# Differences of differential attention and the normed state space output turned by transposing DMAs instead of TensorE

## What is computed

```python
def _ssd_branch(z, ...):                   # y: the state space output, 1024 channels, 2 groups
    yg = (y * jax.nn.silu(z.astype(f32))).reshape(bsz, s, SSD_GROUPS, SSD_WIDTH // SSD_GROUPS)
    yg = yg * lax.rsqrt(jnp.mean(yg * yg, axis=-1, keepdims=True) + EPS)
    return (yg.reshape(bsz, s, SSD_WIDTH) * norm_g.astype(f32)).astype(z.dtype)

def _diff_branch(q, k, v, ...):            # 8 heads, blocks of 128 queries
        sc = jnp.einsum('bqhtd,bkhtd->bhtqk', qi, k) * (HEAD_DIM ** -0.5)
        p = jax.nn.softmax(jnp.where(mask, sc, -jnp.inf), axis=-1)
        attn = p[:, :, 0] - lam * p[:, :, 1]
        return jnp.einsum('bhqk,bkhe->bqhe', attn.astype(v.dtype), v)
```

## Time and profile before

| | |
|---|---|
| median of 3 runs | 1940.49 us (1938.78 to 1941.45) |
| the profiled execution's own time | 1941.98 us |
| its span in the trace | 1940.2 us |
| PE busy | 1914.1 us (99%), granted clock 0.999 |
| DVE busy | 1180.9 us (61%) |
| ACT busy | 996.3 us (51%) |
| POOL busy | 389.1 us (20%) |
| share of the 16 DMA engines | 33.9% |

### The profile page before, as it was taken

One profiled execution on the slowest core, in us unless ns is written; L12 is line 12 of the kernel. 1 busy time (PEld: TensorE's weight loads), 2 busy tenths in 40 slices (PEclk: granted clock), 3 DMA queues, 4 the chain that ended last, 5 costly groups with the idle time before them and its releaser, 6 DMA issues.

```text
span 1940.2 us, 28236 instructions
## 1 busy us (share of the span) xinstructions
PE 1914.1 (99%) x11272; PEld 1044.9 (54%) x11272; DVE 1180.9 (61%) x1555; ACT 996.3 (51%) x1924; POOL 389.1 (20%) x266
## 2 busy tenths in 40 slices
PE   7999999999999999999999999999999999999998
PEld 4446755455455665544454576554554556655443
DVE  6677555587436877644367765655872477775432
ACT  5674454465324666533356644544662256665321
POOL 0212011142212232111001130112331222321110
PEclk9999999999999999999999999999999999999999
DMA  6224223343334443233222242233333443332421
GB/s 190 86 87 153 98 98 109 98 117 96 103 103 126 125 126 109 88 130 137 66 66 87 77 163 94 103 109 91 111 104 109 125 115 105 114 109 88 156 93 44
DMA packets 204525, 208.98 MB, mean 108 GB/s; under 512 B 28688, under 2 KB 193514, under 8 KB 204394
## 3 DMA queue, kind: packets, MB, share of 16 engines
q1 hardware_dynamic: 204394, 207.17, 33.9%
HBM read 181.91 MB, written 2.16 MB: 95 GB/s over the span
## 4 chain that ended last, share of the span: by engine, by line
PE 91%; DVE 3%; issue 2%; ACT 1%; DMA 1%; POOL 1%; SPq 0%; DVEq 0%; POOLq 0%; ACTq 0%
PE PS L558 89%; DVE X L1315 1%; PE PS L750 1%; PE PS L666 1%; DVE wsp L1312 1%; DMA stage<-w_in 1%; PE PS L798 0%; PE PS L806 0%; POOL X L1672 0%; PE PS L836 0%; DMA X<-X 0%; DVE Y L1312 0%; DVE Y L1471 0%; ACT Y L1210 0%; DVE M L1312 0%
## 5 line engine op out<-in xcount | busy, mean ns | idle before, releaser
L558 PE MATMUL PS<-hT,wsp 128*128 128x512 f16 (+2 forms) x4968 | 1085.7, 376 | 1.0 <-ACT hT L966 1.0
L558 PEld LDWEIGHTS PS<-hT,wsp 128*128 128x128 f16 x4968 | 479.1, 98 | 556.4 <-issue 11.9
L1312 DVE SCALAR_TENSOR_TENSOR wsp<-stage,wsp 128x2048 f16<-128x2048 f32 x148 | 352.9, 2385 | 165.5 <-ACT wsp L985 163.3
L558 PE MATMUL PS<-ys,wsp 128*128 128x512 f16 x1536 | 340.4, 379 | 0.0
L985 ACT ACTIVATE wsp<-stage 128x2048 f16<-128x2048 f32 x148 | 281.3, 1901 | 50.6 <-PE PS L558 46.9
L558 PEld LDWEIGHTS PS<-ys,wsp 128*128 128x128 f16 x1536 | 149.4, 98 | 177.0 <-issue 4.1
L558 PE MATMUL PS<-wsp,hT 128*128 128x256 f16 x1728 | 194.2, 273 | 0.0
L558 PEld LDWEIGHTS PS<-wsp,hT 128*128 128x128 f16 x1728 | 168.5, 98 | 22.7 <-issue 2.3
L988 ACT ACTIVATE X<-PS 128x512 f32<-128x512 f32 (+1 forms) x120 | 68.5, 594 | 143.4 <-PE PS L558 122.9
L1672 POOL TENSOR_TENSOR X<-X,K 128x1024 f32<-128x1024 f32 x26 | 63.8, 2452 | 365.5 <-DMA X<-X 365.5
L1001 ACT ACTIVATE G<-PS,halfA 128x512 f32<-128x512 f32 x64 | 43.9, 686 | 161.2 <-PE PS L558 119.1
(11 more groups left out here) (199 smaller groups left out, 2056.9 us busy)
## 6 DMA issues: line engine op xcount, KB each, us to landing
stage<-w_in SPq DMA_DIRECT2D x120, 1024.0 KB, 4.9
stage<-w_branch SPq DMA_DIRECT2D x32, 1024.0 KB, 5.0
X<-X SPq DMA_DIRECT2D x120, 128.0 KB, 2.3
stage<-w_out SPq DMA_DIRECT2D x8, 1024.0 KB, 5.4
Y<-sums SPq DMA_DIRECT2D x8, 512.0 KB, 5.8
M<-sums SPq DMA_DIRECT2D x8, 512.0 KB, 5.7
Y<-Y SPq DMA_DIRECT2D x24, 128.0 KB, 2.3
xres<-x SPq DMA_DIRECT2D x4, 512.0 KB, 6.5
```

What stands on the lines that cost most here:

```text
L558: return pe.matmul(o, a, b, start=start, stop=stop, skip_group_check=True)
L1312: return dve.scalar_tensor_tensor(out=o, in0=a, scalar=c, in1=b, op0=op0, op1=op1)
```

## The change

Both uses of PE transposes go. The differences are written in place (dE), rounded on ACT to a high half and on DVE to a low half side by side in a new f16 buffer dH, and one DMA for each block `n`, issued by SP, transposes both halves at once: 2(i+1) squares of 128 x 128 in f16. For the state space output, DVE now multiplies by the reciprocal norm and by the channel weight, which lies along the free axis as a row loaded to all partitions (`norm_row`); ACT and DVE write the halves into the memory of xs[g], and two DMAs for each group transpose 16 squares each. That memory of group 1 is also used by the first rotated query panel, so ACT waits for all four DMAs (`yb_in`) before it empties slot 28's first bank.

```diff
@@ SP: new
+                def turn_differences(p):
+                    for e in range(2):
+                        n = 2 * (p - DIFF0) + e
+                        halves = 2 * (n % 4 + 1) * P
+                        sp.wait_ge(s["df_hi"], at("df_hi", n + 1, layer))
+                        sp.wait_ge(s["df_lo"], at("df_lo", n + 1, layer))
+                        if n >= 2:
+                            sp.wait_ge(s["df_o"], at("df_o", n - 1, layer))
+                        sp.dma_start_transpose(dPT[:, e, 0:halves].rearrange("p (b n) -> p b n", n=P), dH[:, e, 0:halves])\
+                            .then_inc(df_turned[e], 16)
...
+                def turn_normed(g):
+                    sp.wait_ge(s["yb_hi"], at("yb_hi", g + 1, layer))
+                    sp.wait_ge(s["yb_lo"], at("yb_lo", g + 1, layer))
+                    sp.wait_ge(s["y_lo"], at("y_lo", 8, layer))
+                    for h, y in enumerate((Y_HI[1], Y_LO[1])):
+                        sp.dma_start_transpose(y[:, 4 * g:4 * g + 4, :].rearrange("p t (c n) -> p (t c) n", n=P), turned_z[g][h])\
+                            .then_inc(s["yb_in"], 16)
...
+                    if DIFF0 <= p - 2 < DIFF0 + 16:
+                        turn_differences(p - 2)
+                    if p - 2 in SSD_END:
+                        turn_normed(SSD_END[p - 2])
@@ PE
-                            pe.wait_ge(s["df_a"], at("df_a", n + 1, layer))
-                            for b in range(n % 4 + 1):
-                                last = pe.transpose(PS[:, 4 + 2 * e, P * b:P * b + P], dA[:, e, P * b:P * b + P], ident)
-                            last.then_inc(s["df_T"], 1)
...
-                        pe.wait_ge(s["ssd_norm"], at("ssd_norm", g + 1, layer))
-                        pe.wait_ge(s["ssd_y"], at("ssd_y", 4 * g + 4, layer))
-                        for t in range(4):
-                            for c in range(ST):
-                                last = pe.transpose(PS[:, 4 + t, c * P:c * P + P], z[g][:, c, t * P:t * P + P], ident)
...
-                            pe.wait_ge(s["df_Tl"], at("df_Tl", n + 1, layer))
+                            pe.wait_ge(df_turned[e], at("df_turned0", 16 * (n // 2 + 1), layer))
@@ ACT, ahead of evacuate(p, 0)
+                            act.wait_ge(s["df_a"], at("df_a", n + 1, layer))
+                            if n >= 2:
+                                act.wait_ge(df_turned[e], at("df_turned0", 16 * (n // 2), layer))
+                            copy(dH[:, e, 0:nk], dE[:, e, 0, 0:nk]).then_inc(s["df_hi"], 1)
...
+                        if kind == "qc" and i == 0:
+                            act.wait_ge(s["yb_in"], at("yb_in", 64, layer))
@@ DVE
-                        tt(z[g], z[g], grin.unsqueeze(2).to_broadcast([P, ST, S]), ALU.mult).then_inc(s["ssd_norm"], 1)
+                        for c in range(ST):
+                            last = stt(z[g][:, c, :], z[g][:, c, :], grin[:, c:c + 1], norm_row, ALU.mult, ALU.mult)
...
+                            tt(dH[:, e, nk:2 * nk], dE[:, e, 0, 0:nk], dH[:, e, 0:nk], ALU.subtract).then_inc(s["df_lo"], 1)
```

More of the change, by code:

```diff
@@ L265, in program @@
         sy = X[:, 4096:4608].rearrange("p (e u n) -> p e u n", e=2, u=2)
-        squares = T[:, 0:512]
+        squares, norm_row = T[:, 0:512], T[:, 512:1024]
+        turned_z = [[xs_g.rearrange("p c n -> p (c n)")[:, 1024 * h:1024 * h + 1024].bitcast(F16) for h in range(2)] for xs_g in xs]
         def pair(at):
@@ L702, in before @@
                             if n >= 2:
-                                pe.wait_ge(s["df_Tl"], at("df_Tl", n - 1, layer))
+                                pe.wait_ge(s["df_e"], at("df_e", n - 1, layer))
                             if n >= 4:
@@ L814, in values @@
                             h2, u, i = n // 8, (n // 4) % 2, n % 4
-                            pe.wait_ge(s["df_Tr"], at("df_Tr", n + 1, layer))
                             if n % 8 == 0:
@@ L819, in values @@
                                 pe.wait_ge(s["df_e"], at("df_e", n + 3, layer))
-                            pe.wait_ge(s["df_Tl"], at("df_Tl", n + 1, layer))
+                            else:
+                                pe.wait_ge(s["df_or"], at("df_or", n - 1, layer))
+                            pe.wait_ge(df_turned[e], at("df_turned0", 16 * (n // 2 + 1), layer))
                             for b in range(i + 1):
-                                o, keys, chans = PS[:, 5 + 2 * e, 0:P], slice(P * b, P * b + P), slice(P * u, P * u + P)
-                                mm(o, dPT[:, e, 0, keys], vD[h2 % 2][:, 0, b, chans], b == 0, False)
-                                mm(o, dPT[:, e, 0, keys], vD[h2 % 2][:, 1, b, chans], False, False)
-                                last = mm(o, dPT[:, e, 1, keys], vD[h2 % 2][:, 0, b, chans], False, b == i)
+                                o, chans = PS[:, 5 + 2 * e, 0:P], slice(P * u, P * u + P)
+                                high, low = (dPT[:, e, P * k:P * k + P] for k in (b, b + i + 1))
+                                mm(o, high, vD[h2 % 2][:, 0, b, chans], b == 0, False)
+                                mm(o, high, vD[h2 % 2][:, 1, b, chans], False, False)
+                                last = mm(o, low, vD[h2 % 2][:, 0, b, chans], False, b == i)
                             last.then_inc(s["df_o"], 1)
@@ L1130, in between @@
                             .then_inc(s["dec_ready"], 1)
-                    if DIFF0 <= p < DIFF0 + 16:
-                        for e in range(2):
-                            n = 2 * (p - DIFF0) + e
-                            nk = (n % 4 + 1) * P
-                            act.wait_ge(s["df_T"], at("df_T", n + 1, layer))
-                            if n >= 2:
-                                act.wait_ge(s["df_o"], at("df_o", n - 1, layer))
-                            copy(dPT[:, e, 0, 0:nk], PS[:, 4 + 2 * e, 0:nk]).then_inc(s["df_Tr"], 1)
                 def middle(p):
@@ L1242, in one_layer @@
                     before(p)
+                    differences_hi(p)
                     evacuate(p, 0)
@@ L1428, in decays @@
                         link(dve.tensor_scalar(grin, grin, 1.0 / P, None, ALU.mult))
-                        tt(z[g], z[g], grin.unsqueeze(2).to_broadcast([P, ST, S]), ALU.mult).then_inc(s["ssd_norm"], 1)
+                        dve.wait_ge(s["norm_in"], at("norm_in", 16 * (g + 1), layer))
+                        for c in range(ST):
+                            last = stt(z[g][:, c, :], z[g][:, c, :], grin[:, c:c + 1], norm_row, ALU.mult, ALU.mult)
+                        last.then_inc(s["ssd_norm"], 1)
                 def before(p):
@@ L1555, in middle @@
                         g = SSD_END[p]
-                        for t in range(4):
-                            f = 4 * g + t
-                            dve.wait_ge(s["yb_hi"], at("yb_hi", f + 1, layer))
-                            stt(Y_LO[1][:, f, :], PS[:, 4 + t, :], colB[:, B_NG + f:B_NG + f + 1], Y_HI[1][:, f, :], ALU.mult, ALU.subtract)\
-                                .then_inc(s["yb_lo"], 1)
+                        dve.wait_ge(s["yb_hi"], at("yb_hi", g + 1, layer))
+                        tt(by_columns(turned_z[g][1]), z[g].rearrange("p c (t n) -> p t c n", n=P), by_columns(turned_z[g][0]), ALU.subtract)\
+                            .then_inc(s["yb_lo"], 1)
                     if p in DIFF_END:
```

74 lines of the change are left out of this document (37 added, 37 removed).

## The result

| | before | changed |
|---|---|---|
| median | 1939.86 us (4 runs, 1938.78 to 1941.45) | 1916.47 us (4 runs, 1912.84 to 1917.38) |
| ratio, 95% interval | 1 | 0.9876 [0.9861, 0.9892] |
| span of the profiled run | 1940.2 us | 1914.8 us |

What follows compares the result with a forecast made beforehand. PE, busy 99% of the span, was taken to bound the kernel. 28.0 us removed less 5.3 us displacement gave 22.7 us off; from 1940.5 that forecast 1917.8, say 1918 us, range 1911 to 1924 (chance 0.42).

Steps and rivals of the forecast that it cites:

- What goes (28.0): On PE: 160 difference transposes 17.4 us, 64 state space output transposes 7.2, wait for normed z 3.4; sum 28.0 us.
- The displacement (5.3): Slots 54 and 58, both layers: moved copies delay rotation, POOL, head norm, exponentials; 4 x (1.0 + 0.33) = 5.3 us.
- rival (d): Low halves also fall behind POOL; DVE cost 14 us, total 1927; chance 0.14 together with (a) at 6.9 to 9 us.
- The pair of DMAs (5.6): Even slots: two transposing DMAs, 14 squares, priced from Y<-T at 1.75 x 2.5 + 1.2 = 5.6 us, hidden.
- room 6.9 us: Slot 54: time from first low half at 680.9 until values of slot 55 need the pair at 687.8.
- The break-even of rival (a) (9.3 us a pair): Even slots: pair length at which PE's waits at the values use up the gain of 22.7 us; 0.66 us a square.
- rival (a): Transposing DMAs are slow and PE waits at the values; up to 14.2 us a pair, 2056; chance 0.24 beyond 9.5 us.
- my formula: For a pair of x us, PE stands x - 6.9 in 6 slots and x - 8.4 in the 10 other even ones.
- They keep their time: The rotation's four moves behind the pair on SP: issue time unchanged, landing up to 2 us later.
- The state space output: Transposes 7.2 us and wait 3.4 us go; group 1's DMAs land in 11.2 us, holding ACT 7 us, hidden from PE.

Runs made afterwards that it cites:

- Experiments 4 and 5: Changed kernel with copies of the differences back at their old places: both ACT's and DVE's 1929.6 us (4); only ACT's 1929.69, only DVE's 1927.16 us (5).
- experiment 3: Changed kernel with the second block's transposing DMA of each pair issued, waited for and issued again: 1956.05 us, ratio 1.0079 to the kernel before.
- experiment 1: Kernel before with only half the change: transposing DMAs for the differences alone 1927.29 us, for the state space output alone 1928.4 us.

## Why the prediction was right, and where it was not

**What goes (28.0).** Right in size. PE's busy time fell by 23.5 us for the 24.6 forecast, and the stall of 3.4 us went with it. What I missed is a further 2.6 us of PE's waits on the low halves in PSUM; the row was in the view of waits from which I took the 1.9 us of the earlier trace rows. Against the 25.4 us of span the forecast of 22.7 is 2.7 us short, by these waits and by the next term; only the medians, 23.4 us apart, make it look nearer.

**The displacement (5.3).** The direction is right; that the total came near is luck, for the reason given was mostly wrong. PE's waits on exponentials grew by 3.8 us, and in slots 54 and 58 they are 0.24 and 1.04 us in layer 0 and 1.01 and 0.40 in layer 1, 2.7 us in place of four times 1.6; the other 3.0 us fell in slots 50, 52 and 56. Two steps failed. The first is that the copies ahead of the rotation's high halves on ACT start them 1.0 us later. In slot 53 the copies took 0.60 us (from 654.34) and ACT had time for them: the high halves then waited 1.93 us for DVE's sum of the rotation and started 0.1 us behind its end, as they had before:

```profile
658.73 2.14 ACT L1003 ACTIVATE X<-X 64x1024 f16<-64x1024 f32 x2 [1.93 <-DVE X L1338]
```

It is the sum that was late, 1.4 us when counted from the values of the slot (4.7 us behind their start in place of 3.3), and its moves on SP had begun 1.7 us later by the same count, behind the pair. The second is that DVE stands behind POOL at the head norm and moves with it by 1.0 us: POOL started 0.2 us after DVE's low halves and stood itself, and the head norm ran its plain 1.22 us. Of the 3.0 us outside slots 54 and 58, 2.7 us lie in the slots right behind the three in which a low half stood behind POOL (0.62 and 0.22 us in slots 50 and 52 of layer 0, 0.83 and 1.04 us in slot 50 of layer 1). That is the collision of rival (d), in other slots than it had named; that it makes these waits is read from their places and was not tried.

Worse, I held the old place to be the cheap one. Experiments 4 and 5 show that low halves which read SBUF cost 11 to 13 us there; that this is near the 14 of rival (d) is chance, since (d) counted four slots at the new place.

**The pair of DMAs (5.6).** Measured 1.2 + 3.1 = 4.3 us, with the length from experiment 3. In the changed kernel's own profile the pair of slot 54 had landed 4.4 us after it was issued, and that of slot 52, with a longer issue, 5.0 us. The nearest row, Y<-T, was the right one to go by. The issue was 1.2 us instead of the 0.6 taken from plain moves, and a square cost 0.16 us behind a base of 1.8, instead of a cost in proportion to the pieces. The first low half of slot 54 was done at about 673.15 (SP issued at 673.19) and the values of slot 55 began at 680.07: room 6.9 us, as forecast.

**The break-even of rival (a) (9.3 us a pair).** Wrong for a pair that also holds SP. With some 3.0 us more, at about 7.3 us a pair, the kernel lost 39.6 us, where my formula has 6 x (7.3 - 6.9) = 2.4. By a straight line between the two measurements (an estimate) the gain of 23.4 is used up at 4.3 + 3.0 x 23.4/39.6 = 6.1 us. The formula priced only the values, which lost 8.4 us. It left out the rotation's moves that stand behind the pair in SP's queue (11.6 us at the scores and 10.6 us at the splits; I had written that a late sum only pushes a split that is one slot ahead of PE), and what PE's clock loses. By this line the margin was 1.8 us a pair, and not 3.7, so the chance of (a) deserved more weight than I could see. Data that are slow while SP goes on issuing is another case; it was not run.

"VectorE: DVE Perf Modes" (The three transpose paths) of the Trainium skill gives 1309 ns for one bf16 square by DMA. As the price of a chain of squares (f16 here) the runs refute it: 8 squares had landed 3.07 us after issue. "DMA: Bandwidth & Descriptors" (Latency and other measured facts) of the Trainium skill has 261 GB/s for transposing DMAs; four further squares of 32 KB in 0.64 us are 205 GB/s in this kernel (an estimate from two lengths), beside other traffic, a fifth below it.

**The rotation's moves.** "They keep their time" failed in the trace: SP began those for slot 53 at 650.39, behind the pair, 1.7 us later against the values than before (the prediction allowed up to 2 us, but for the landing). DVE's waits for POOL at the sum of the rotation grew from 16.6 to 35.9 us in total; not all of this is lateness, since DVE had stood behind POOL in the instruction ahead of the sum before (eight times some 2.1 us, now twice). PE did not wait for a panel split, as forecast.

**The state space output.** The half is worth 12.4 us for the 10.6 forecast (7.2 + 3.4); 2.3 us of the 12.4 are the waits that became shorter in experiment 1. Group 1's DMAs were issued at 358.42 instead of 362.6 and had landed 6.9 us later instead of 11.2. ACT stood 5.75 us ahead of slot 28's first bank where I had 7, and PE waited for nothing:

```profile
365.32 0.60 ACT L1003 ACTIVATE X<-PS 128x512 f32<-128x512 f32 x1 [5.75 <-DMA ys<-X]
```

## What to carry to other kernels

Where PE is busy for 99% of the span, price what leaves it by the starts in its timeline, and price a new DMA by its issue, by a base and a rate, and by everything that stands behind it in its queue and by what waits for that: here it was not the weight loads but the small moves of the rotation that cost. When an operand moves from PSUM to SBUF, look up what GpSimd does at that moment: the same two VectorE instructions took 0.6 us when they came first and 2.2 to 2.5 us when one of them came second. Its place in the program is part of the change, on both engines that have to move.

## What the runs showed that I had not expected

- A transposing DMA within SBUF (f16, 128 x 128 squares) held SP for 1.2 us with 2 to 8 squares (2.0 to 2.4 us now and then) and, in the slot shown, 1.54 us with 14; with 16 in the state space output the median was 2.3 us.
- 4 squares had landed 2.43 us and 8 squares 3.07 us after issue, in slots 53 and 54 of experiment 3.
- VectorE and GpSimd lengthened each other, by order of start: 0.62 to 2.19 us and 4.32 to 5.65 us; a VectorE instruction with an operand in PSUM kept its 0.68 us. In the kernel before, a scaling of 256 columns within SBUF that started together with GpSimd's took 2.51 us in place of 0.35.
- A wait of PE of 2.84 us was followed by a granted clock of 0.79 over 8 us, and 24 matmuls took 7.04 instead of 5.34 us; behind waits of 2.44 and 2.52 us in the same run the next 24 took 5.35.
- The four moves landed 5.3 us after issue from ACT's queue and 2.3 us from SP's (medians), in the first case with a load of 1 MB issued on SP between them.
